# Turning the right half of x before its inverse roots are known, and multiplying them in afterwards in PSUM

## What is computed

```python
def rmsnorm(x, w):
    xf = x.astype(jnp.float32)
    y = xf * lax.rsqrt(jnp.mean(xf * xf, axis=-1, keepdims=True) + EPS)
    return (y * w.astype(jnp.float32)).astype(x.dtype)
...
        h = rmsnorm(x, norm1_w[l])
        proj = jnp.einsum('bsd,dp->bsp', h, w_in[l])
```

## Time and profile before

| | |
|---|---|
| median of 3 runs | 408.76 us (408.75 to 408.99) |
| the profiled execution's own time | 409.83 us |
| its span | 407.8 us |
| PE busy | 402.3 us (99%) |
| PEld busy | 346.0 us (85%) |
| DVE busy | 304.2 us (75%) |
| ACT busy | 263.4 us (65%) |
| POOL busy | 48.2 us (12%) |

### The profile page before, as it was taken

The page is one execution under the profiler, slowest core; times in us unless marked ns, Lnnn a source line. Parts: engine busy times, 40 slices in busy tenths (PEclk is TensorE's granted clock), DMA queues, the critical chain, the costliest instruction groups (busy, mean ns, idle before and its releaser), DMA issues.

```text
span 407.8 us, 6020 instructions
## 1 busy us (share of the span) xinstructions
PE 402.3 (99%) x2257; PEld 346.0 (85%) x2257; DVE 304.2 (75%) x445; ACT 263.4 (65%) x363; POOL 48.2 (12%) x30
## 2 busy tenths in 40 slices
PE   8999999999999999999999999999999999999996
PEld 7998888788888888888888888888888888888885
DVE  3989869767756889879766677877677767776775
ACT  6978888885399765797536675654554565535540
POOL 3106976411011000000004000000000000000000
PEclk9999999999999999999999999999999999999999
DMA  7845773684462622236555346645545555455202
GB/s 294 320 163 203 268 291 117 253 232 169 165 252 104 206 104 104 103 111 215 199 198 178 134 156 236 219 168 218 169 175 206 206 206 182 141 203 199 98 2 103
DMA packets 12644, 74.09 MB, mean 182 GB/s; under 512 B 1336, under 2 KB 2768, under 8 KB 4432
## 3 DMA queue, kind: packets, MB, share of 16 engines
q1 hardware_dynamic: 12616, 73.81, 50.8%
q10 hardware_dynamic: 8, 0.00, 0.0%
HBM read 72.74 MB, written 1.07 MB: 181 GB/s over the span
## 4 chain that ended last, share of the span: by engine, by line
PE 83%; DVE 8%; ACT 3%; DMA 3%; issue 1%; SPq 1%; ACTq 0%; DVEq 0%
PE pj L1537 23%; PE pj L1538 13%; PE pj L1496 7%; PE pj L1498 7%; PE pj L1497 7%; PE mx L1498 6%; PE mx L1497 6%; PE mx L1496 6%; PE mx L1562 5%; DVE acc L1012 4%; DMA w_b<-in_w_in 3%; PE mx L1559 2%; ACT whi L453 1%; PE pj L1540 1%; DVE wlo L925 1%
## 5 line engine op out<-in xcount | busy, mean ns | idle before, releaser
L1537 PE MATMUL pj<-hT,whi 128*128 128x512 f32 x474 | 166.3, 394 | 0.0
L925 DVE TENSOR_TENSOR wlo<-w_b,whi 128x2048 fp32r<-128x2048 f32 x55 | 126.0, 2291 | 45.3 <-ACT whi L453 45.3
L1538 PE MATMUL pj<-hT,wlo 128*128 128x256 f32 x496 | 138.8, 280 | 0.0
L453 ACT CAST whi<-w_b 128x2048 fp32r<-128x2048 f32 x63 | 120.2, 1907 | 27.5 <-PE pj L1498 21.4
L1537 PEld LDWEIGHTS pj<-hT,whi 128*128 128x128 f32 x474 | 88.8, 187 | 19.8 <-DVE acc L1012 0.3
L1538 PEld LDWEIGHTS pj<-hT,wlo 128*128 128x128 f32 x496 | 93.6, 189 | 1.3 <-issue 0.3
L413 POOL TENSOR_TENSOR wlo<-w_b,whi 128x2048 fp32r<-128x2048 f32 x8 | 37.1, 4639 | 117.4 <-ACT whi L453 97.1
L841 ACT COPY st_b<-pj 128x512 f32<-128x512 f32 x22 | 12.9, 587 | 40.4 <-PE pj L1538 40.4
L1496 PE MATMUL pj<-whi,hT 128*128 128x512 f32 x96 | 38.2, 398 | 0.0
L1498 PE MATMUL pj<-whi,hT 128*128 128x512 f32 x96 | 37.5, 390 | 0.0
L1497 PE MATMUL pj<-wlo,hT 128*128 128x512 f32 x96 | 37.4, 389 | 0.0
(11 more groups left out here) (286 smaller groups left out, 595.9 us busy)
## 6 DMA issues: line engine op xcount, KB each, us to landing
w_b<-in_w_in SPq DMA_DIRECT2D x23, 1024.0 KB, 4.9
w_b<-in_w_up SPq DMA_DIRECT2D x22, 1024.0 KB, 4.8
w_b<-in_w_down SPq DMA_DIRECT2D x11, 1024.0 KB, 4.8
w_b<-in_w_out SPq DMA_DIRECT2D x8, 1024.0 KB, 4.8
seg_b<-ld_rows SPq DMA_DIRECT2D x4, 512.0 KB, 6.7
x_pad<-in_x SPq DMA_DIRECT2D x2, 512.0 KB, 3.7
w_b<-in_w0c SPq DMA_DIRECT2D x1, 512.0 KB, 7.4
Wm_b<-m_rows_d SPq DMA_DIRECT2D x1, 512.0 KB, 5.7
```

The lines of the kernel that those rows point to most:

```text
L453: nc.scalar.copy(whi[:, slot, :], wraw[:, slot, :]).then_inc(s.hi_done, 1)
L925: nc.vector.tensor_tensor(wlo[:, slot, :], wraw[:, slot, :], whi[:, slot, :].bitcast(F32), ALU.subtract).then_inc(s.lo_done, 1)
L1537: ins = nc.tensor.matmul(ps, whi[:, slot, w], hT[:, k, :, :], start=k == 0, stop=False, skip_group_check=True)
L1538: ins = nc.tensor.matmul(ps[:, 0:T], wlo[:, slot, w], hT[:, k, 0, :], start=early, stop=k == KD - 1, skip_group_check=True)
```

## The change

PE's idle matmuls go from 12 to 9. Behind them, the right half of x is turned raw, straight from `x_sb`, as each token tile lands, and so ahead of `turn_first` and not between k = 0 and k = 1. The two scalings into `xn` (ACT L792, DVE L1340) go. In their place PE multiplies ones by the two diagonals (`spread_first_roots`), which gives a 128 x 256 tile in PSUM whose every partition holds the inverse roots of all tokens; ACT copies it to SBUF (`rbc`); and DVE multiplies the four turned blocks in `pj[1]` by it in place (`scale_right`, 128 x 1024). ACT's `h_hi(4)` waits for that product. DVE's program has `piece_lo(0, 1)` and `h_lo(1)` ahead of `scale_right`, and k = 2 and 3 behind it.

```diff
+        roots_home = bank[3][:, T:2 * T]
...
             def h_hi(c):
-                act.wait_ge(s.hT_ps, c + 1 if c < 4 else KD)
+                if c < 4:
+                    act.wait_ge(s.hT_ps, c + 1)
+                else:
+                    act.wait_ge(s.right_scaled, 1)
...
-            nc.scalar.activation(xn[:, 0, D // 2:D], x_sb[:, 0, D // 2:D], ACT.Copy, scale=stat[:, 2:3]).then_inc(s.xn_first, 1)
             act.wait_ge(s.w0_in0, 16)
             h_hi(0)
             h_hi(1)
             piece_hi(0, 1)
+            act.wait_ge(s.root_ps, 1)
+            nc.scalar.copy(rbc[:, :], roots_home).then_inc(s.root_copied, 1)
             h_hi(2)
...
+            def scale_right():
+
+                dve.wait_ge(s.raw_ps, NT)
+                dve.wait_ge(s.root_copied, 1)
+                v = pj[1][:, :].rearrange("p (c t) -> p c t", c=4)
+                nc.vector.tensor_tensor(v, v, rbc[:, :].unsqueeze(1).to_broadcast([P, 4, T]), ALU.mult).then_inc(s.right_scaled, 1)
...
             h_lo(0)
-            nc.vector.tensor_scalar(xn[:, 1, right], x_sb[:, 1, right], stat[:, 3:4], None, ALU.mult).then_inc(s.xn_second, 1)
-            for k in (1, 2, 3):
+            piece_lo(0, 1)
+            h_lo(1)
+            scale_right()
+            for k in (2, 3):
                 piece_lo(0, k)
                 h_lo(k)
...
                 for c in range(4, KD):
-                    ins = transpose(turned_home(c)[:, t * P:(t + 1) * P], xn[:, t, c * P:(c + 1) * P])
-                    if t == NT - 1:
-                        ins.then_inc(s.hT_ps, 1)
+                    ins = transpose(turned_home(c)[:, t * P:(t + 1) * P], x_sb[:, t, c * P:(c + 1) * P])
+                ins.then_inc(s.raw_ps, 1)
+
+            def spread_first_roots():
+
+                for t in range(NT):
+                    ins = mm(roots_home[:, t * P:(t + 1) * P], ones[:, :], rdiag[:, t, :])
+                ins.then_inc(s.root_ps, 1)
...
                 for k in range(4):
-                    if k == 1:
-                        pe.wait_ge(s.xn_first, 1)
-                        turn_right(0)
-                        pe.wait_ge(s.xn_second, 1)
-                        turn_right(1)
...
+                    if k == 0:
+                        spread_first_roots()
...
-            for _ in range(12):
+            for _ in range(9):
                 mm(bank[3][:, 0:P], ones[:, :], ones[:, :])
             pe.wait_ge(s.consts, 4)
+            pe.wait_ge(s.x_in0, 16)
+            turn_right(0)
+            pe.wait_ge(s.x_in1, 16)
+            turn_right(1)
             turn_first()
```

More of the change, by code:

```diff
@@ L182, in build @@
         names = """x_in0 x_in1 par_in w24_in consts wdma0 wdma1 wdma2 hi_done lo_done lo_pool unit_done
-            w0_in0 w0_in1 w0_in2 w0_first w0_hi w0_lo w1_hi w1_lo ssq0_left ssq0_right ssq1_left ssq1_right root_inv diag0 diag1 rt1 xn_first xn_second hT_ps hi_T lo_T w24_hi w24_lo small_ps rows_copied rows_gates gates_in
+            w0_in0 w0_in1 w0_in2 w0_first w0_hi w0_lo w1_hi w1_lo ssq0_left ssq0_right ssq1_left ssq1_right root_inv diag0 diag1 rt1 raw_ps root_ps root_copied right_scaled hT_ps hi_T lo_T w24_hi w24_lo small_ps rows_copied rows_gates gates_in
             rows_abs rows_e rows_v rows_l expa_r rows_mx rows_kept mb_spread ldb_even ldb_odd rows_ex rows_sc cols_ps cols_ready
@@ L1316, in h_lo @@
                                                in1=hT_hi[:, c, :].bitcast(F32), op0=ALU.mult, op1=ALU.subtract).then_inc(s.lo_T, 1)
-            right = slice(D // 2, D)
+            def scale_right():
[3 more added lines that the diff above has]
+                nc.vector.tensor_tensor(v, v, rbc[:, :].unsqueeze(1).to_broadcast([P, 4, T]), ALU.mult).then_inc(s.right_scaled, 1)
             def part_of_mean(t, ready, done):
```

## The result

The change makes the kernel slower by 0.64 us: 409.49 us (409.19 to 409.92) against 408.85 (408.42 to 409.67), medians of 22 runs each on the same chips, ratio 1.0015 with a 95% interval of 1.0009 to 1.0021. The forecast was 409.2 in a range of 408.3 to 410.1. The profiled execution of the changed kernel, 409.51 us with a span of 407.5, is on the other hand 0.3 us *shorter* than the profiled one of before, and how both can be true is the main lesson of this study.

A forecast was written before the change was run, and what follows sets the result against it. The ACT and DVE chain from ACT's split of unit 2 to `xs_turn` at 64 us was taken as the bound, PE close behind. PE 0, ACT +0.45, DVE 0 gave 409.2 us, range 408.3 to 410.1.

The forecast's parts named there:

- The mechanism: ACT and DVE chain from unit 2's split: PE's 0.27 us is waited off, ACT's delay moves the end one for one.
- case A: The forecast itself: ACT's chain is later by 0.2 to 0.7 us, giving 409.0 to 409.5; chance 0.55.
- The ACT term (+0.45): Wait and roots' copy before the third h_hi: ACT's split of unit 2 starts at 16.45, not 16.02; ends 0.2 and 0.6.
- The cover: ACT's idle before the split at 16.02, 0.38 to 0.5 us until unit 2 lands, takes up part of ACT's delay.
- case B: Without the profiler unit 2 may land half a microsecond later and hide ACT's delay: 408.7 to 408.9; chance 0.13.
- case E: Unit 2 lands by 15.5 (term 0.95) or the product takes 2.3 us (term 1.1): 409.7 to 409.9; chance 0.12.
- the removed scaling: ACT's 128 x 512 scaling between 7.07 and 7.97: removing it gives nothing, as PE's turned block releases the first h_hi.
- The PE terms: Idle matmuls and raw turns cost 0; the stream from 8.83 makes PE 0.27 us earlier at k = 1, no gain.
- A sign of being wrong that appeared: On PE in the changed profile: passes behind 5.5 us that are 0.21 apart would show the prediction wrong.
- The DVE term (0): DVE's in-place PSUM product takes 1.15 us, and its 0.85 us delay fits its idle plus ACT's 0.45: cost 0.
- C, the clock: PE's clock rises only after the left half is turned, ACT's term grows by 1.9: 411.1 (+0.6%); chance 0.12.
- D: PE's stream is the time, so its 0.27 us and small waits come back: 408.3 to 408.6; chance 0.08.

The follow-up runs named there:

- Run 2: The changed kernel without the spreading matmuls, the copy of the roots and the product, so the right half lacks its inverse roots: 409.01 us, ratio 1.0000 to before.
- runs 6 and 7: The kernel before (6) and the changed kernel (7), each with an extra 512 KB load ahead of unit 2's load: 410.79 us, 1.0049, and 410.82 us, 1.0042.
- the repeat of before: The kernel before, unchanged, run again for a second profile (also called run 1): 408.86 us, ratio 1.0001.
- run 11: The changed kernel with the 4 KB gate-rows DMA issued by SyncE behind unit 5 and not by ScalarE: 409.58 us, ratio 1.0013 to before.
- run 9: The changed kernel with the load of par (115 KB) behind unit 2's load and not ahead of it: 409.44 us, ratio 1.0016 to before.
- run 3: The changed kernel with the copy of the roots on DVE, behind its second low piece, and not on ACT: 409.75 us, ratio 1.0023 to before.
- run 12: The kernel before with the gate-rows DMA issued by SyncE and par's load behind unit 2's: 408.48 us, ratio 0.9987 to before.
- run 8: The kernel before with the load of par (115 KB) behind unit 2's load and not ahead of it: 408.74 us, ratio 0.9996 to before.
- run 4: The changed kernel with the two spreading matmuls ahead of unit 0's first group and not behind it: 409.42 us, ratio 1.0008 to before.
- run 10: The kernel before with the 4 KB gate-rows DMA issued by SyncE behind unit 5 and not by ScalarE: 408.48 us, ratio 0.9990 to before.

## Why the prediction was right

**The mechanism.** The forecast was that PE's gain is waited off and that ACT's delay at the split of unit 2 moves the end one for one. Run 2 shows the first (0.9 us earlier on PE, nothing at `xs_turn`), the table the second, and runs 6 and 7 that the price vanishes when the landing covers it. The shift of the median was to be 0.45 and was 0.64; at 409.49 it lies at the upper edge of case A's range of 409.0 to 409.5. That the number came this close is in part luck: two errors inside the term, of 0.17 and of about 0.3 us, went against each other.

**The ACT term (+0.45) was mis-sized, in two parts.** The delay of ACT itself was put at 0.95 us. In the changed profile the cast before it starts at 8.56 and would hand over 0.51 later, at 9.07; the copy starts at 9.58 and gives way at 9.85. That is 0.51 of waiting and 0.27 of copy, 0.78 in all. The copy was budgeted at 0.4 with `h_hi`'s duration and costs 0.27 from start to start (0.37 long); the estimate of 0.51 from the Trainium skill's "ScalarE: Activation LUTs" (section "Rules for kernel authors") was further off, and that budget is for an ACTIVATE with a pointer operand as its bias, which this copy does not have. The cover was put at 0.4 to 0.5 us before the split, from the idle time before 16.02. In the repeat of before ACT's last piece starts at 14.31 and would hand over at 14.83 to 14.85, and the split starts at 15.02: 0.17 to 0.19 of cover. 0.78 - 0.17 = 0.61, against 0.64 measured. Unit 2 landed between 14.66 and 15.00 in the early profiles, and ACT was ready at 14.83, so even this cover is the largest of them. In an execution with a late landing the two kernels are 0.18 us apart at the split (16.20 in run 11, whose program up to there is the change's, and 16.02), where the working said 0.45: the copy at 10.14 was within 0.1 us of the forecast 10.2, the third `h_hi` at 10.41 in place of 10.6.

So the step that failed is the one that took the landing at 16.02 as the kernel's own. It was that of one execution, of the rarer kind. The text named the landing without the profiler as unknown, but put more weight on a later one (case B, 0.13) than on an earlier one (half of case E, 0.12). It is earlier: case B is wrong, and the truth lies between A and E.

**A row was misread.** "0.19 us of idle before 7.97, ended by PE" was the ground for giving nothing for the removed scaling. POOL's cast in that execution starts at 8.07 behind the same load for which `h_hi(0)` also waits (`w0_in0`), and the rows of run 6, whose head is that of before, name the DMA at 7.93. It was the landing. The conclusion held by luck: in the repeat `h_hi(0)` starts at 7.81 behind the scaling and in the change at 7.83 behind PE, so the removed 0.71 us bought nothing there either.

**The PE terms.** 0 for the raw turns: right; they ran from 5.07 to 6.46 and held the left half back by about 0.1 us. -0.27 on the stream: PE was 0.4 earlier at `small_proj` than in the repeat (14.65 against 15.04), since the four passes of the roots cost 0.37 start to start (8.93 to 9.30) and not 0.52. It was waited off at units 3 to 5 and `xs_turn`. The new wait came at unit 3, for DVE's split, which I had not named: against the repeat PE goes from 0.39 us early to 0.07 late there, loses some 0.3 us more at unit 4 and 0.16 at the start of unit 5, where the prediction had put 0.9.

**A sign of being wrong that appeared.** PE passes behind 5.5 us that are 0.21 apart were to show the prediction wrong, and in the changed profile they are 0.21 apart until 6.13. The sign was badly chosen and not the mechanism wrong: run 9, where the spacing halved at 4.8, has the same split and the same time.

**The DVE term (0).** The product was put at 1.15 and took 1.13 start to start. DVE kept 0.29 us of idle before its split, where I expected 0.47. It is no cost beside ACT's, and it leaves so little room that run 3 could not gain.

**The rivals.** C, the clock, is refuted by runs 2 and 9; no run shows a rise as late as it needed, behind the whole left half. What the Trainium skill says in "TensorE: Matmul & The Clock Gate" (section "Part 4: PE-mode transpose"), that transposes do not count as PE-busy in the way matmuls do, is neither shown nor contradicted: in the changed profile the spacing of the passes halved during the transposes, at about 6.1 us, but by then 18 idle passes had run. D is refuted by run 2. E was right in its first half, the early landing, with 0.64 in place of 0.95.

## What to carry to other kernels

Before reading a difference of half a microsecond out of two profiles, profile the unchanged kernel twice and compare the landings of the first loads: here they differed by 1.5 us between executions, and the pair of profiles had the wrong sign. Idle time that ends at a DMA's landing is cover only in the executions in which the landing is late, so it belongs into the range and not into the sum. And where two engines stand within 0.3 us of each other at the same point, work taken from PE, or handed from one to the other, gained nothing here; what helped (0.39 us) was a DMA issue taken out of the chain behind that point.

## What the runs showed of the hardware that I had not expected

**The clock's rise is not tied to the program.** The idle passes tell the moment at which their spacing goes from 0.21 to 0.11 us, the levels of 1.2 and 2.4 GHz. The same 24 took 4.97 and 5.33 us in two profiles of one program and 5.49 in run 12; 18 of them took 4.21 in the change, 4.03 in run 9 with the same program on PE, and 3.61 in run 3. The spacing halved at 5.3 and at about 6.1 us in the two profiles of before, at 6.1 in the change and at 4.8 in run 9; the ends are 3.9 (run 3) and 7.1 (run 12). The granted clock over the span was recorded as 0.998 to 1.000 in all of them. In most profiles I see no cost: a wait for a diagonal comes behind the rise, or the first `h_hi` starts as early as where it does (7.81 in the repeat of before and 7.83 in the change, with rises at 6.1; 7.86 in run 9, with one at 4.8). Run 12 is the exception:

```profile
8.19 0.84 ACT L777 ACTIVATE hT<-mx,w_b 128x256 fp32r<-128x256 f32 x2 [0.30 <-PE mx L1566]
```

Its scaling started at 7.18, and `h_hi` follows the scaling by 0.74 to 0.75 us in the repeat of before and in run 8, so PE's slow passes of the left half held ACT back by 0.26 us (an estimate from these rows). Unit 2 had landed at 14.34 and the split started at 15.21 without a wait, so nothing took this up.

**A small DMA behind large ones.** The 4 KB of gate rows, issued at 21.3 in run 4 and waited for until 25.90, took over 4 us; in run 10 it was issued at 20.7 and waited for until 24.27. In the runs where it was late, DVE's last piece of unit 1 was late too, and with it the issue of unit 4's load of 1 MB; that the one delays the other fits, but was not tried by itself. The rows also go with unit 5's load: DVE's wait for them ended at 25.96, 25.90, 24.27, 25.63 and 24.56 in runs 3, 4, 10, 11 and 12, and unit 5's 1 MB landed at 26.02, 25.63, 24.10, 25.35 and 24.44. In the change it landed at 24.84, ahead of 25.19, when DVE came for the rows, and there was no wait.

**The tail varies.** DVE's last addition and the span, of run 1 and of run 2:

```profile
core 0 of [0], span 406.8 us
...
403.49 0.49 DVE L1479 SCALAR_TENSOR_TENSOR x_pad<-pj,stat,x_pad 128x256 f32<-128x256 f32 x1 [0.23 <-PE pj L1498]
```

```profile
core 0 of [0], span 408.3 us
...
403.47 0.49 DVE L1489 SCALAR_TENSOR_TENSOR x_pad<-pj,stat,x_pad 128x256 f32<-128x256 f32 x1 [0.23 <-PE pj L1508]
```

The last instruction that computes is at the same place, and the span differs by 1.5 us, all of it in the landing of the output: its last DMA took 2.4 us in the first and 3.9 in the second. The span of a single profile is therefore no measure for changes of this size; the start of a late instruction is.
